# Expert scores on TensorE: passes of 512 and of 256 columns, in blocks or alternating one by one

## What is computed

```
q      = x1 @ w_pq                       # keys are scored, 16 of 16384 experts are
idx, g = top-k of the key scores         # picked per token and head, with gates g
act    = gelu(einsum('thkd,td->thk', expert_u[idx], x1))
ffn    = einsum('thk,thkd->td', g * act, expert_v[idx])
out    = layer_norm(ALPHA * x1 + ffn)
```

## Time and profile before

| | |
|---|---|
| Time, three runs | 1880.57 us median (1880.29 to 1881.3) |
| Time of the profiled execution | 1882.42 us |
| Span in its trace | 1880.6 us |
| TensorE busy | 1854.2 us (99%) |
| Weight loads | 1575.0 us (84%) |
| VectorE busy | 1539.4 us (82%) |
| GpSimd busy | 1047.7 us (56%) |
| ScalarE busy | 1006.5 us (54%) |
| Expert scores, first to last pass | 558.7 to 1276.4 us |
| Expert values | from 1276.4 us on |

### The profile page before, as it was taken

The page is one execution under the profiler, slowest core; times in us unless marked ns, Lnnn a source line. Parts: engine busy times, 40 slices in busy tenths (PEclk is TensorE's granted clock), DMA queues, the critical chain, the costliest instruction groups (busy, mean ns, idle before and its releaser), DMA issues.

```text
span 1880.6 us, 33239 instructions
## 1 busy us (share of the span) xinstructions
PE 1854.2 (99%) x9326; PEld 1575.0 (84%) x9326; DVE 1539.4 (82%) x2157; ACT 1006.5 (54%) x1842; POOL 1047.7 (56%) x769
## 2 busy tenths in 40 slices
PE   9999999999999999999999999999999999999996
PEld 7888888887888888888888888887888888888885
DVE  4555676767579988999999999996999888888887
ACT  4455555544565665555555555555555555555553
POOL 0000231200488989888878875556788666665523
PEclk9999999999999999999999999999999999999998
DMA  7777776565868677799999999997999999999993
GB/s 231 231 239 227 241 236 202 185 204 148 211 184 213 193 190 199 177 196 197 243 233 195 193 194 252 260 273 248 361 384 362 388 342 348 401 377 368 381 340 90
DMA packets 329197, 476.50 MB, mean 253 GB/s; under 512 B 93712, under 2 KB 224976, under 8 KB 328304
## 3 DMA queue, kind: packets, MB, share of 16 engines
q1 hardware_dynamic: 258288, 391.62, 67.9%
q0 software_dynamic: 52416, 80.02, 15.5%
q10 hardware_dynamic: 18432, 4.20, 1.2%
HBM read 453.41 MB, written 21.07 MB: 252 GB/s over the span
## 4 chain that ended last, share of the span: by engine, by line
PE 95%; DVE 3%; DMA 1%; ACT 0%; POOL 0%; issue 0%; SPq 0%; ACTq 0%; DVEq 0%
PE ps L763 25%; PE ps L516 14%; PE ps L518 14%; PE ps L517 14%; PE ps L769 13%; PE ps L803 6%; PE ps L804 6%; DVE split_lo L1263 0%; PE ps L506 0%; PE ps L733 0%; DVE x_cols L1485 0%; DMA raw<-in_w_out 0%; DVE act_both L1276 0%; DMA x_nat<-in_x 0%; DMA act_dram<-halves 0%; DVE stats L1834 0%
## 5 line engine op out<-in xcount | busy, mean ns | idle before, releaser
L763 PE MATMUL ps<-act_both,split_hi 128*128 128x512 f32 x2048 | 513.2, 392 | 0.0
L763 PEld LDWEIGHTS ps<-act_both,split_hi 128*128 128x128 f32 x2048 | 368.4, 189 | 65.8
L1192 ACT ACTIVATE v_hi<-v_tile 128x1024 fp32r<-128x1024 f32 x248 | 263.3, 1063 | 255.5 <-PE ps L804 251.7
L1784 DVE TENSOR_TENSOR v_lo<-v_tile,v_hi 128x1024 fp32r<-128x1024 f32 x248 | 309.8, 1272 | 81.3 <-ACT v_hi L1192 81.1
L1263 DVE TENSOR_TENSOR split_lo<-raw,split_hi 128x512 fp32r<-128x512 f32 x304 | 232.6, 771 | 162.0 <-ACT split_hi L859 161.0
L859 ACT ACTIVATE split_hi<-raw 128x512 fp32r<-128x512 f32 x344 | 216.4, 631 | 227.6 <-PE ps L518 224.9
L1982 POOL DMA_INDIRECT gate_dram<-pick_n,places x192 | 296.0, 1542 | 61.8 <-issue 61.8
L1072 ACT ACTIVATE split_hi<-ps 128x512 fp32r<-128x512 f32 x368 | 209.1, 594 | 220.8 <-PE ps L769 220.8
L2030 POOL DMA_INDIRECT rows<-in_expert_v,picked x128 | 211.7, 1654 | 159.4 <-DVE row_sum L1796 119.7
L769 PEld LDWEIGHTS ps<-act_both,split_lo 128*128 128x128 f32 x2048 | 279.5, 190 | 20.0
L769 PE MATMUL ps<-act_both,split_lo 128*128 128x256 f32 x2048 | 285.9, 282 | 0.0
(11 more groups left out here) (209 smaller groups left out, 2431.9 us busy)
## 6 DMA issues: line engine op xcount, KB each, us to landing
raw<-in_expert_u SPq DMA_DIRECT2D x1024, 128.0 KB
v_tile<-in_expert_v SPq DMA_DIRECT2D x256, 512.0 KB, 7.1
raw<-in_w_in SPq DMA_DIRECT2D x112, 512.0 KB
raw<-in_w_out SPq DMA_DIRECT2D x32, 512.0 KB
raw<-in_w_pq SPq DMA_DIRECT2D x128, 128.0 KB
gate_dram<-zeros SPq DMA_DIRECT2D x24, 512.0 KB, 5.8
gates<-gate_dram POOLq DMA_DIRECT2D x64, 192.0 KB, 7.2
act_dram<-halves ACTq DMA_DIRECT2D x128, 32.0 KB
```

Source lines behind the costliest of these rows:

```text
L763: return nc.tensor.matmul(ps[:, bank, :], split_hi[:, q % SPLITS, i * P:(i + 1) * P], act_both[:, k, :, :].rearrange("p a t -> p (a t)"), ...
L1192: nc.scalar.activation(v_hi[:, unit % UNITS, :], v_tiles[unit % RING][:, :], ACT.Copy).then_inc(v_hi_ready, 1)
L1784: vec.tensor_tensor(v_lo[unit % RING][:, :], v_tiles[unit % RING][:, :], v_hi[:, unit % UNITS, :].bitcast(f32), ALU.subtract).then_inc(v_l ...
```

## The change

```diff
-                for n in range(4):
-                    t, two = n // 2, (2 * n, 2 * n + 1)
-                    if n % 2 == 0 and not (isinstance(pair, int) and pair < 2):
+                for t in range(2):
+                    if not (isinstance(pair, int) and pair < 2):
                         pe.wait_ge(score_free, pair * 2 + (t - 1))
-                    for q in two:
+                    bank = first + t
+                    pe.wait_ge(hi_ready, pair * 8 + (Q_U + 4 * t + 1))
+                    for i in range(4):
+                        wide(bank, 4 * t, i)
+                    for q in range(4 * t + 1, 4 * t + 4):
                         pe.wait_ge(hi_ready, pair * 8 + (Q_U + q + 1))
-                        for i in range(3 if q % 4 == 3 else 4):
-                            wide(first + t, q, i)
-                    for q in two:
-                        pe.wait_ge(lo_ready, pair * 8 + (Q_U + q + 1))
+                        pe.wait_ge(lo_ready, pair * 8 + (Q_U + q))
                         for i in range(4):
-                            last = narrow(first + t, q, i)
-                        if q % 4 == 3:
-                            last = wide(first + t, q, 3)
+                            last = narrow(bank, q - 1, i)
+                            if q % 4 < 3 or i < 3:
+                                wide(bank, q, i)
                         last.then_inc(split_free, 1)
                         if after:
-                            after(q)
+                            after(q - 1)
+                    q = 4 * t + 3
+                    pe.wait_ge(lo_ready, pair * 8 + (Q_U + q + 1))
+                    for i in range(4):
+                        narrow(bank, q, i)
+                    wide(bank, q, 3).then_inc(split_free, 1)
+                    if after:
+                        after(q)
```

## The result

| | before | after |
|---|---|---|
| Median of six runs, us | 1880.79 | 1888.38 |
| Lowest and highest, us | 1879.98, 1881.3 | 1886.7, 1893.93 |
| Profiled execution, its time and its span, us | 1882.42, 1880.6 | 1887.69, 1885.9 |

The change makes the kernel slower: the ratio is 1.0041, with a 95% interval of 1.0024 to 1.0058, so 7.6 us by the medians. I had predicted 1878.5 us, 2.1 us less than before. The measured time lies inside the range that I gave for 8 in 10 (1869 to 1891 us), but on its slower side, to which I gave 0.30.

The account below looks back on a forecast made before the run. TensorE was taken as the bound, never idle in the expert scores, so pass steps set the time. Order -2.2 us and late low parts +0.1 gave -2.1 us: 1878.5 us against the median of 1880.57, range 1869 to 1891.

Parts of the forecast that it names:

- part 1: Pass order in the expert scores: a single narrow-wide pair takes 347 ns, a tile 5.570 us against 5.587, 2.2 us less.
- a loan and its payment: At width changes, the 6 ns a first narrow pass gives back cancel the 6 to 7 ns the next wide takes.
- upper bound: Slowest step allowed for a single wide pass between narrow ones: 235 ns, the slowest of a run.
- rival B: Disturbance never settles among single score passes: pair 355 ns, tile 5.658 us, 9.1 us more, 1889.8 us; slower side's chance 0.32.
- point of decision: Single-pair time in the expert scores at which the change does nothing: 348.5 ns; above it the kernel is slower.
- step 2: Low parts needed up to 0.92 us earlier in the score stage; supply mostly keeps up, 0.1 us counted.
- the place named: Tightest supply point, about 702 us, where ACT loads tables and POOL stands: 0.88 us in hand, 0.92 wanted.
- step 3: TensorE's waits for high and low parts, two now side by side, and pair 0's hook passes: cost zero.
- step 4: Stall and slow clock behind the scores may change: 1.5 us either way, zero in the sum.
- Rival A: Single wide score pass is undisturbed: pair 340.5 ns, tile 5.499 us, 11.3 us less, 1869.4 us; chance 0.32 including cases between.
- Rival C: Score-pass order does nothing, or supply or clock takes 2 us back: within 0.2%, 1880.6 us; chance 0.06.
- my middle: Middle of the bounds set for a single narrow-wide pair in the expert scores, 340.5 and 355 ns.

Follow-up runs that it names:

- second and third experiment: Changed kernel with its alternating passes regrouped into runs of four (second, ratio 1.0016) and runs of two, NNWW (third, 1.0004), ratios to the kernel before.
- the first experiment: Changed kernel with the same alternating order, but the wait for the high part moved one pass later, so no two waits adjoin; ratio 1.0041 to the kernel before.

## Why the prediction was wrong

**The step that failed is the price of the single pair in part 1.** I took the narrow pass at 114 ns as behind a settled wide one and the wide pass at 233 as first behind a settled narrow run, 347 together, and called the two a loan and its payment. In the changed kernel the pair is 353 ns. The 6 ns between them, in 11 x 128 pairs, are 8.4 us, nearly all of the 9.1 us from this part's forecast (2.2 us less) to the measured stage (6.9 us more); 353 is rounded. Durations within the tile show both halves wrong:

```profile
L763 PE MATMUL ps<-act_both,split_hi 128*128 128x512 f32 x1 | 0.4, 403 | 0.0
L769 PE MATMUL ps<-act_both,split_lo 128*128 128x256 f32 x1 | 0.3, 284 | 0.0
L763 PE MATMUL ps<-act_both,split_hi 128*128 128x512 f32 x1 | 0.4, 398 | 0.0
L769 PE MATMUL ps<-act_both,split_lo 128*128 128x256 f32 x1 | 0.3, 278 | 0.0
L763 PE MATMUL ps<-act_both,split_hi 128*128 128x512 f32 x1 | 0.4, 395 | 0.0
L769 PE MATMUL ps<-act_both,split_lo 128*128 128x256 f32 x1 | 0.3, 281 | 0.0
```

The rows are three pairs in a row, from 1000.25 to 1001.30 us, and the order then repeats. Less 163, the narrow passes step 121, 115 and 118 ns, not 114 each: two of three give back little. The wide ones step 240, 235 and 232, 236 on average, above even my upper bound of 235. This is the side of rival B, at three quarters of its price: B had 9.1 us more than before, measured are 6.9. It isn't B in full, as a third of the narrow passes still give back their 5 to 6 ns and one wide pass in three goes beyond B's 235. Its point of decision, 348.5 ns, was right, and 353 lies beyond it.

**The reading of a loan and its payment was argued, not shown, and the pairs refute it.** If the narrow pass lent what the wide one behind it pays, an alternating pair would have no surplus at any width. It has 6 ns at 256, 5 at 320 and 12 at 384. With it falls the reason for which I let the two cancel.

**The two numbers were both read in a state that the change removes.** The 114 was read with seven or more wide passes ahead, the 233 with eight narrow ones. The prediction said that neither had a row for a single pass, and took the nearest. The same fault is in the expectations of the second and third experiment, which were 1.7 and 2.2 us too high. Steps read behind long runs gave too low a price for single passes and too high a one for runs of two and four. The traces show that the price varies with what came before, three values in turn when alternating; why it does they don't show.

**What held.** The run of five narrow passes takes 0.60 us, predicted 0.593, and the five wide passes 1.16. Supply held (step 2) but for one small delay: TensorE had one late low part, at the place named (700.87 us here, as the stage begins earlier). The timeline there:

```profile
699.82 1.09 PE L763 MATMUL ps<-act_both,split_hi 128*128 128x512 f32 x4
...
700.87 0.36 PE L769 MATMUL ps<-act_both,split_lo 128*128 128x256 f32 x1
701.07 0.40 PE L763 MATMUL ps<-act_both,split_hi 128*128 128x512 f32 x1
```

The second to fifth wide pass behind a run take 0.93 us elsewhere (1.16 less 0.23), and here the narrow one begins 1.05 us after the first of them; it then steps 0.20 us instead of 0.12. Together 0.2 us are lost, where I had counted 0.1. One number of that step was off, without effect: piece 1's slot comes free three wide passes later, 0.7 us and not 0.9. The waits side by side cost nothing (step 3), as the first experiment shows. The end of the stage (step 4) came out the other way, to the change's advantage. TensorE idled for 3.08 us there, more than the 2.37 of the earlier trace rows, and yet kept its clock:

```profile
1294.04:1297.50 3.46, 3.46 (x15) 2.89 (x16) 3.46 (x4) 2.96 (x5) 2.85 (x3) 1.00 0.96 359
```

The granted clock is 1.00 behind the stall, where it was 0.53 before. So the 1.5 us of slow clock are saved and 0.7 us more are idle: 0.8 us net, within the 1.5 us either way of the prediction. TensorE's last stall, for the low part before the final products, takes 0.6 us of it back (4.0 us, and 3.4 before); the value products and the end are 0.9 us longer in all. **Rival A** is excluded: its condition was that one narrow pass builds no backlog, and its pair of 340.5 ns is 13 below the measured one. **Rival C** is excluded too: the interval of the ratio, 1.0024 to 1.0058, lies above its 0.2%.

**Open.** What a change of width does inside TensorE isn't settled. The runs exclude the waits, the alternation of operands alone, the half of the PSUM bank that the narrow passes sum into, and, at 320 columns and above, a load that doesn't fit under the pass. They don't say why the surplus is 5 to 6 ns at 256 and 320 and 12 at 384, why runs of two are cheaper than runs of four, nor why the same run costs more or less by what stood before it. Two things weren't varied: one of the two widths was always 512 columns, and all passes of a tile sum into one bank, so that it matters how soon a column is summed into again stays possible.

## What to carry to other kernels

Where TensorE is the bound and never idle, read the distance from start to start of the passes, and measure the pattern that you mean to use. A step read in a settled stream doesn't price a pass in a stream that never settles, and bounds read there don't either: my middle, 347.8 ns, was still on the wrong side of 348.5, and single wide passes lay beyond the upper bound. The number of changes doesn't price an order: seven narrow runs per tile cost 46 ns and four cost 56. Of the orders tried here, the one with the longest runs was cheapest per tile, as far as the parts that it needs could be made in time.

## What the runs showed of the hardware

- Behind eight narrow passes of 256 columns the wide passes need five to settle (1.16 us, then 0.91 for four). At 320 columns a run costs the same 20 ns as at 256 (stage of 772.1 us).
- In a run, passes of 192 columns with a weight load each step 110 ns, and not the 93 of their columns. When such a pass stands alone between wide ones it steps 0.08 us, and the wide pass behind it takes 0.26 us instead of 0.23.
- The surplus of an alternating pair goes up and down with the narrow width: 6 ns at 256, 5 at 320, 12 at 384, 0 at 512.
- The price of the same four passes NNWW changes with their place in the tile: 0.71, 0.70, 0.70 and 0.69 us in order, undisturbed 0.693.
- A stall of 3.08 us left the granted clock at 1.00, and one of 2.37 us in the kernel before was followed by 0.53. The length of a stall alone doesn't tell whether the clock falls.
